# Layer 0's modulation products moved between the chunks of the first block's FFN, all modulation kept as columns

## The reference

```python
for l in range(DEPTH):                                   # DEPTH = 2
    mod_x = (silu(c) @ ada_w[l] + ada_b[l])[:, None, :]   # ada_w[l]: 1024 x 6144
    mod_c = silu(c_ctx) @ ada_w[l] + ada_b[l]
    sh1, sc1, g1, sh2, sc2, g2 = jnp.split(mod_x, 6, axis=-1)
    csh1, csc1, cg1, csh2, csc2, cg2 = jnp.split(mod_c, 6, axis=-1)
    hx = rms_norm(x, norm_g[l, 0]) * (1 + sc1) + sh1
    ...
    x = x + g1 * rms_norm(yx, norm_g[l, 1])
```

## Time and profile before

| | us |
|---|---|
| median of 3 runs | 3338.43 |
| lowest, highest | 3336.55, 3341.86 |
| the profiled execution | 3342.58 |
| its span in the trace | 3340.4 |
| PE busy in it | 2973.3 (89%) |
| DVE busy | 1865.6 (56%) |
| ACT busy | 1396.6 (42%) |

### The profile page before, as it was taken

The page is one execution under the profiler, slowest core; times in us unless marked ns, Lnnn a source line. Parts: engine busy times, 40 slices in busy tenths (PEclk is TensorE's granted clock), DMA queues, the critical chain, the costliest instruction groups (busy, mean ns, idle before and its releaser), DMA issues. The chain is left out here.

```text
span 3340.4 us, 38468 instructions
## 1 busy us (share of the span) xinstructions
PE 2973.3 (89%) x15372; PEld 2271.3 (68%) x15372; DVE 1865.6 (56%) x2265; ACT 1396.6 (42%) x1786; POOL 13.5 (0%) x13
## 2 busy tenths in 40 slices
PE   6999599795899999999999789999778998889797
PEld 4799498675667676676676544548667776757796
DVE  3555444334788887888888530205444554345675
ACT  3211244232666666676666411213133333343554
POOL 0000000000000000000000000000000000000000
PEclk9999799897899999999999888899679999999898
DMA  4300245331798898998899895120012222210352
GB/s 156 135 1 1 76 152 183 133 114 66 297 350 331 339 350 320 348 347 329 340 352 344 321 420 197 57 76 4 1 51 84 88 89 76 88 45 20 122 188 76
DMA packets 95036, 589.98 MB, mean 177 GB/s; under 512 B 20464, under 2 KB 21488, under 8 KB 25488
## 3 DMA queue, kind: packets, MB, share of 16 engines
q1 hardware_dynamic: 91840, 581.22, 46.4%
q10 hardware_dynamic: 3024, 6.33, 0.5%
HBM read 586.46 MB, written 1.05 MB: 176 GB/s over the span
## 5 line engine op out<-in xcount | busy, mean ns | idle before, releaser
L1807 DVE TENSOR_TENSOR s_w_low<-weight_ring,s_w_high 128x2048 fp32r<-128x2048 f32 x336 | 759.6, 2289 | 136.9 <-ACT s_w_high L1746 133.0
L1746 ACT ACTIVATE s_w_high<-weight_ring 128x2048 fp32r<-128x2048 f32 x336 | 629.7, 1908 | 139.1 <-PE bank L1727 116.5
L248 DVE TENSOR_TENSOR s_w_low<-weight_ring,s_w_high 128x1024 fp32r<-128x1024 f32 x238 | 289.3, 1221 | 200.0 <-ACT s_w_high L233 199.9
L1727 PE MATMUL bank<-s_w_high,s_x_low 128*96 128x512 f32 x896 | 364.1, 406 | 7.6 <-DVE s_w_low L1807 7.6
L233 ACT ACTIVATE s_w_high<-weight_ring 128x1024 fp32r<-128x1024 f32 x238 | 249.6, 1052 | 282.8 <-PE bank L490 282.8
L490 PE MATMUL bank<-s_x_high,s_w_low 128*128 128x256 f32 (+1 forms) x1056 | 341.1, 323 | 29.4 <-DVE s_w_low L248 29.4
L1727 PE MATMUL bank<-s_w_high,s_x_high 128*96 128x512 f32 x896 | 359.1, 401 | 0.0
L1727 PE MATMUL bank<-s_w_low,s_x_high 128*96 128x512 f32 x896 | 357.3, 399 | 0.0
L490 PE MATMUL bank<-s_x_low,s_w_high 128*128 128x256 f32 (+1 forms) x1056 | 339.5, 321 | 0.0
L490 PE MATMUL bank<-s_x_high,s_w_high 128*128 128x256 f32 (+1 forms) x1056 | 339.2, 321 | 0.0
L344 PE MATMUL bank<-s_w_high,s_x_low 128*128 128x512 f32 x544 | 220.2, 405 | 56.8 <-DVE s_w_low L248 56.8
(11 more groups left out here) (437 smaller groups left out, 4297.6 us busy)
## 6 DMA issues: line engine op xcount, KB each, us to landing
weight_ring<-moe_w SPq DMA_DIRECT2D x336, 1024.0 KB, 6.3
weight_ring<-ada_w SPq DMA_DIRECT2D x48, 1024.0 KB, 12.8
weight_ring<-ffn_up SPq DMA_DIRECT2D x44, 1024.0 KB, 4.8
weight_ring<-ffn_w_in SPq DMA_DIRECT2D x22, 1024.0 KB, 4.8
weight_ring<-ffn_down SPq DMA_DIRECT2D x22, 1024.0 KB, 4.8
weight_ring<-ffn_w_down SPq DMA_DIRECT2D x11, 1024.0 KB, 4.8
weight_ring<-w_rkv_cols SPq DMA_DIRECT2D x8, 1024.0 KB, 8.2
weight_ring<-moba_qk SPq DMA_DIRECT2D x8, 1024.0 KB, 4.8
```

What stands on the lines that cost most here:

```text
L248: K.nc.vector.tensor_tensor(self.lo[:, b, :], self.source(c, i), self.hi[:, b, :], ALU.subtract)\
L1727: last = nc.tensor.matmul(o, xs[:, e % 2, k, :], ws[:, b, c], start=(k == 0 and m == 0), stop=(k == KT - 1 and m == 2))
L1746: nc.scalar.activation(halves(whi, kind, n, i), raw(kind, n, i), ACT.Copy).then_inc(S["high"].h, 1)
L1807: V.tensor_tensor(halves(wlo, kind, n, i), raw(kind, n, i), halves(whi, kind, n, i), ALU.subtract)\
```

## The change

1. The 24 chunks of layer 0 are taken out of `adaln` and put into the FFN phase, two after each group's up chunk, and four after the last group. The step's products run between the groups on PE (`steps[0]`), ACT copies the bank after the next silu (`steps[1]`), and every vector, gates included, is turned to columns by four matmuls a step. The columns are kept in `modulation_columns`.
2. For this, the FFN's two outputs of a chunk share one bank (the other banks go to the modulation), and a chunk's four parts run in another order: both halves of the rows for the first 128 outputs, then for the second.
3. silu of the conditions is formed at the head of the FFN phase, and their load is issued as the program's first DMA; both leave `moe`.
4. `adaln` keeps 12 steps (layer 1), with the gates first (`KIND`). The repeated bias and gain rows are no longer loaded: gates are added and multiplied as columns (8 values wide), and a row is then made by 8 matmuls of a repeated column against the identity (`row`) and two copies by DVE (`keep`). PE waits for the small loads before its first step, for the gate columns after the step b = 2, for kept rows at b = 4 and b = 7. The layer norm's square roots are asked from ACT after its copies b = 2 and b = 3. The modulation of the transposed tokens is put into the copy out of the bank.
5. A small table and two small buffers of a later stage are laid over `modulation_columns` and `condition_wide`.

```diff
--- before.py
+++ after.py
@@ gated_hidden, tensor
                 for s in range(2):
-                    for i in range(2):
-                        pe.wait_ge(*parts.low.at(4 * c + 2 * s + i + 1))
+                    for n in range(4):
+                        i, h = (n % 2, n // 2) if steps else (n // 2, n % 2)
+                        if n == 0 or (i and n < 3):
+                            pe.wait_ge(*parts.low.at(4 * c + 2 * s + i + 1))
...
+                        if h:
+                            last.then_inc(*(K.used if i else parts.half).up())
                     K.taken += 1
+                if steps:
+                    for b in (c,) if c < chunks - 1 else (c, c + 1):
+                        steps[0](pe, b)
+            if steps:
+                steps[0](pe, None)
@@ gated_hidden, scalar
+            if steps:
+                steps[3](act)
             for q in range(0, KT, 2):
                 nc.scalar.activation(xhi[:, q:q + 2, :], x[:, q:q + 2, :], ACT.Copy).then_inc(*xsplit.up())
...
                     last.then_inc(*gated.up())
+                    if steps and c:
+                        steps[1](act, c - 1)
@@ modulation_steps
+    def tensor(pe, b):
+        if b == 0:
+            pe.wait_ge(*cond_made.at(1))
+        if b is not None:
+            if b >= 2:
+                pe.wait_ge(*copied.at(b - 1))
+            for c in range(2):
+                w = K.chunk(pe).rearrange("p (k n) -> p k n", k=KT)
+                for k in range(KT):
+                    r = slice(k % 4 * 32, k % 4 * 32 + 32)
+                    last = nc.tensor.matmul(K.ps[4 + b % 2][r, c * 256:c * 256 + 256], K.wide[:, k, :], w[:, k, :],
+                                            start=(k < 4), stop=(k >= 4))
+                last.then_inc(*K.used.up())
+        n = 11 if b is None else b - 1
...
+        pe.wait_ge(*copied.at(n + 1))
+        for j in range(4):
+            o = 8 * n + 2 * j
+            last = nc.tensor.matmul(K.ps[6][:, o:o + 2], mod[:, n % 2, j * P:(j + 1) * P], K.pick[:, :],
+                                    start=True, stop=True)
+        last.then_inc(*spread.up())
...
+    def begin(act):
+        act.wait_ge(*cond_in.at(16))
+        nc.scalar.activation(K.wide[:, :, 0:2], K.cond[:, :, :], ACT.Silu).then_inc(*cond_made.up())
@@ adaln, tensor
+                def row(r, bank):
+                    for h in range(2):
+                        for m in range(4):
+                            j = 4 * h + m
+                            last = nc.tensor.matmul(K.ps[bank + h][:, m * P:(m + 1) * P],
+                                                    bc(gcol[:, r, j:j + 1], [P, P]), K.ident[:, :], start=True, stop=True)
+                        last.then_inc(*row_made.up())
+
+                pe.wait_ge(*cols_in.at(48))
...
+                    if b:
+                        columns(b - 1)
+                    if b == 2:
+                        pe.wait_ge(*gates_made.at(1))
+                        row(0, 0)
+                        row(1, 2)
+                    if b == 4:
+                        pe.wait_ge(*row_kept.at(2))
+                        row(2, 0)
+                        pe.wait_ge(*row_kept.at(4))
+                        row(3, 2)
+                    if b == 7:
+                        pe.wait_ge(*row_kept.at(8))
+                        turn(0)
+                        turn(1)
@@ adaln, scalar
-                root_of_norm(0)
-                for b in range(24):
+                for b in range(12):
...
+                    if b in (2, 3):
+                        root_of_norm(b - 2)
+                    if b == 4:
                         square(2, 0)
                         square(3, 1)
@@ adaln, sync
-                for n in range(4):
-                    load(K, sp, grb[:, n, :], i["ada_b_gates"][n].partition_broadcast(P))
-                    load(K, sp, gng[:, n, :], i["norm_g_gates"][n].partition_broadcast(P))
@@ build
-        chunks("ffn_w_in")
+        for c in range(FF // 256):
+            chunks("ffn_w_in", 2 * c, 2 * c + 2)
+            chunks("ada_w", 2 * c, 2 * c + 2)
+        chunks("ada_w", 22, 24)
...
-        chunks("ada_w")
+        for kind in (2, 5, 0, 1, 3, 4):
+            chunks("ada_w", 24 + 4 * kind, 28 + 4 * kind)
```

More of the change, by code:

```diff
@@ L195, with __init__ @@
 class Split:
-    def __init__(self, K, st, chunks, depth, rows=None):
-        self.K, self.first, self.rows = K, K.taken, rows
+    def __init__(self, K, st, chunks, depth, rows=None, where=lambda c: c):
+        self.K, self.first, self.rows, self.where = K, K.taken, rows, where
         self.chunks, self.depth, self.nact, self.ndve = chunks, depth, 0, 0
@@ L212, in source @@
     def source(self, c, i):
-        return self.K.ring[:, (self.first + c) % R, i * CH // 2:(i + 1) * CH // 2]
+        return self.K.ring[:, (self.first + self.where(c)) % R, i * CH // 2:(i + 1) * CH // 2]
     def at(self, c, i):
@@ L223, in act @@
             c = self.nact
-            n = self.first + c
+            n = self.first + self.where(c)
             act.wait_ge(K.landed[n % R], 16 * (n // R + 1))
@@ L228, in act @@
                 if c >= self.depth:
-                    act.wait_ge(*(K.used if i else self.half).at(c - self.depth + 1))
+                    act.wait_ge(*(K.used.at(self.where(c - self.depth) + 1) if i else self.half.at(c - self.depth + 1)))
                 if self.rows:
@@ L452, in layer_norm, with gated_hidden @@
         K.v(dve, nc.vector.tensor_tensor(flat, flat, b, ALU.add))
-def gated_hidden(K, st, x, hid, chunks, conv=None):
+def gated_hidden(K, st, x, hid, chunks, conv=None, steps=None):
     nc = K.nc
@@ L465, in gated_hidden @@
     centre, tapped, gated, free, xsplit, xlow = K.sig(6)
-    parts = Split(K, st, 2 * chunks, 1 if tok > T else 2)
+    where = (lambda c: c + 2 * (c // 2)) if steps else (lambda c: c)
+    parts = Split(K, st, 2 * chunks, 1 if tok > T else 2, where=where)
     K.uniq += 1
@@ L527, in _ @@
                 silu(chunks - 1)
+            if steps:
+                steps[1](act, chunks - 1)
+                steps[1](act, chunks)
         @block.vector
@@ L536, in product @@
                 last.then_inc(*free.up())
+            if steps:
+                steps[4](dve)
             for q in range(0, KT, 2):
@@ L561, in _ @@
                 product(chunks - 1)
+            if steps:
+                steps[2](dve)
             dve.wait_ge(*free.now())
@@ L566, in _, with modulation_steps, scalar, pick @@
             K.stream(sp)
+def modulation_steps(K, st, first):
+    nc = K.nc
+    V = nc.vector
+    cond_in, cond_made, picked, copied, spread = (K.early[n] for n in ("cond_in", "cond_made", "picked", "copied", "spread"))
+    mod, = scratch(K, st, [P, 2, 512])
+    out = K.columns[:, 0].rearrange("p q j w -> p (q j w)")
+    def tensor(pe, b):
[12 more added lines that the diff above has]
+        n = 11 if b is None else b - 1
+        if n < 0:
+            return
+        if n == 0:
+            pe.wait_ge(*picked.at(1))
+        pe.wait_ge(*copied.at(n + 1))
[4 more added lines that the diff above has]
+        last.then_inc(*spread.up())
+    def scalar(act, b):
+        act.wait_ge(*K.used.at(2 * min(b, 10) + 2 + 2 * b + 2))
+        if b >= 2:
+            act.wait_ge(*spread.at(b - 1))
+        nc.scalar.activation(mod[:, b % 2, :], K.ps[4 + b % 2][:, :], ACT.Copy).then_inc(*copied.up())
+    def pick(dve):
+        for who in range(2):
+            last = V.reduce_sum(K.pick[:, who:who + 1],
+                                K.ident[:, :].rearrange("p (q n) -> p n q", q=4)[:, who:who + 1, :], AX)
+        K.v(dve, last, picked)
+    def vector(dve):
+        dve.wait_ge(*spread.at(12))
+        K.v(dve, V.tensor_copy(out, K.ps[6][:, 0:96]))
+    def begin(act):
+        act.wait_ge(*cond_in.at(16))
+        nc.scalar.activation(K.wide[:, :, 0:2], K.cond[:, :, :], ACT.Silu).then_inc(*cond_made.up())
+    return tensor, scalar, vector, begin, pick
 def rwkv_front(K, units, cols, bones, hsel, bonus, dstate, edge, loads):
@@ L1920, in root_of_norm @@
                     nc.scalar.activation(rs[:, :], rs[:, :], ACT.Sqrt).then_inc(*norm_root.up())
[L1922 to L1923 removed]
+                for b in range(12):
                     act.wait_ge(*K.used.at(2 * b + 2))
[L1925 to L1930 removed]
+                    if b == 8:
+                        act.wait_ge(*spread.at(8))
+                        for n in range(2):
+                            last = nc.scalar.activation(K.columns[:, 1, 2 + 3 * n, :, :].rearrange("p j w -> p (j w)"),
+                                                        K.ps[6][:, 32 + 48 * n:48 + 48 * n], ACT.Copy)
+                        last.then_inc(*shifted.up())
+                    if b >= 2:
+                        act.wait_ge(*spread.at(b - 1))
+                    nc.scalar.activation(mod[:, b % 2, :], K.ps[4 + b % 2][:, :], ACT.Copy).then_inc(*copied.up())
+                    if b in (2, 3):
+                        root_of_norm(b - 2)
```

(3 more changed lines are left out.)

279 lines of the change are left out of this document (140 added, 139 removed).

## The result

| | us |
|---|---|
| before, median of 4 runs (lowest, highest) | 3339.66 (3336.55, 3341.86) |
| after, median of 4 runs (lowest, highest) | 3308.93 (3303.17, 3313.85) |
| ratio, with its 95% interval | 0.9905 (0.9890 to 0.9921) |
| profiled executions, before and after | 3342.58, 3303.17 |
| their spans | 3340.4, 3301.3 |

The forecast was 3313 with a range of 3301 to 3327. The four runs lie in two pairs, 3303 and 3304 against 3313 and 3314, and the profile is of a run of the lower pair. The profiled difference, 39.4 us, is therefore more than the medians' 30.7.

The account below looks back on a forecast made before the run. The prediction took `adaln` to be bound by weight transfers and the FFN by PE. Its terms, 35.1 - 59 - 1.3 = -25.2 us, took the profiled 3342.58 to 3317.4, or a median of 3313, range 3301 to 3327.

Parts of the forecast that it names:

- The FFN, +35.1: FFN phase: PE has no idle time, so the added matmuls lengthen it by 35.1 us, head, seams and tail included.
- head: Start of the FFN phase: ACT's table load and silu of the conditions before x is split, +1.5 us.
- seams: FFN: 23 changes between fp32r and step matmuls, 0.5 us allowed in all, 2.3 if each cost 0.1 us.
- tail: End of the FFN phase: DVE's last product is covered, a copy of 96 values takes its place, -0.5 us.
- `adaln`, -59: `adaln`: a chain of waits among PE, ACT and DVE replaces the transfer bound, ending at 76.4 us; 59 us shorter.
- Small terms, -1.3: Outside FFN and `adaln`: conditions' load leaving a list -0.45, exp table load running ahead -1.3, program's first DMA +0.5 us.
- The router stage: Router's phase: conditions' load leaves a waited list, -0.45 us, and exp's table load no longer waits for DVE, -1.3 us.
- The program's start: Program's head: the conditions' load is the first DMA, so all behind it comes 0.45 us later, taken as +0.5.
- The clock in the FFN: Rival: thin steps lower PE's clock at FFN seams; 3373 us for the whole (3%), 3344 for steps only (4%).
- The chain's slow end: Rival in `adaln`: waits invite the slow clock, gain of 43 us in place of 59, 3329 us; 13%.
- the fast end: Rival in `adaln`: the clock rises early and stays, gain of 67 us, 3305 us; 10%.
- The ring: Rival in the FFN: the third close transfer lands 1 us late in every group, 3324 us; reserve about 8 us, 2%.

Follow-up runs that it names:

- e5: The kernel before the change, unaltered, run and profiled again: 3343.52 us.
- e11: The kernel before the change with 25 DVE memsets (3.11 us) added at the end of the router's phase: 3340.63 us.
- the repeat: The changed kernel, unaltered, run again: median of four runs 3302.11 us, ratio 0.9879 to the kernel before.
- e4: The changed kernel with the four column matmuls of each of the FFN's twelve steps made four times over: 3363.26 us.
- e6: The changed kernel with the layer norm's two square roots in `adaln` asked one step earlier: 3296.93 us in one run.
- e7: The changed kernel with PE's wait for the bias columns in `adaln`, and the bias matmul, moved behind the second step: 3309.72 us in one run.

## Why the prediction was right

**The FFN, +35.1: measured +35.0.** From the start of the transposition phase to the next phase's first matmul it was 144.3 us (413.66 to 557.95), now 179.3 (415.67 to 594.96). The parts: head 10.80 against 9.42, +1.4 (forecast 1.5); from the first FFN matmul to PE's end +34.5 (forecast 33.6, and 0.5 of seams); tail 4.72 against 5.56 of waiting, -0.8 (-0.5). A step is 1.86 and 0.92 us, as sized from `adaln`; each seam to and from an fp32r matmul costs 0.08 to 0.09 us over their regular 0.12. That is some 1.9 us for 23 seams, the mis-sized term here: near the 2.3 that the prediction named as the alternative, and not the 0.5 that it took. What offset it is luck: behind the first FFN matmul PE ran at 1.2 GHz for 4.0 us and not for 5.3, which gave back 0.65. The sum is sounder than its first decimal, though: the phase is 143.7 to 144.3 us in the four profiles without the move, and 178.8 to 179.5 in the eight with the phase as in after. The groups are 14.45 us apart (products at 453.50 and 467.95), 14.3 by the forecast.

**`adaln`, -59: measured -64.7.** The chain was the right one, link for link, with no wait for `ada_w`. Most links were forecast a little long, in us from the start of the phase:

| | forecast | measured |
|---|---|---|
| first step | 3.9 | 3.3 |
| step 2's products done | 13 | 11.1 |
| first root | 15.4 | 13.3 |
| first norm | 19 | 17.0 |
| gate columns | 20.8 | 18.5 |
| rows 0 and 1 | 26.8 | 24.5 |
| second root | 29.8 | 27.1 |
| second norm, four copies | 36.2 | 33.4 |
| rows 2 and 3, step 5 | 43 | 39.6 |
| squares | 46.3 | 42.5 |
| kept rows | 50.4 | 46.2 |
| PE's end | 74.1 | 69.8 |
| last coefficient | 76.4 | 71.3 |

No link is far off, and nearly all errors have one sign. The largest is the first three steps, 7.8 us instead of 9: the slow clock cost less there than I took (64 records in 4.93 us, then one step at 1.93). The start is 0.6 us shorter. The root, from the products' end to its own, is 2.2 us for 2.4. The strings of tiny DVE operations start 0.1 to 0.2 us apart, so twelve coefficients take 1.5 us, not 2.3. For the rows 0 and 1 the slow clock was sized well (5.95 us, 6 forecast), and so was PE alone at the end (23.6, 23.7). One error cost nothing: DVE places a half tile in 1.3 us (16 operations in 5.20) and not in 0.9, which is slower than `turn`, but a step stands between the two pairs of `turn` and hides it.

**Small terms, -1.3.** The router stage gave -2.6 for -1.8. The mechanism is seen (the table load at 855.19 ahead of its wait), but the size is not fixed: the nine kernels with this edit and no memsets have 185.1 to 187.9 us there, and without the time at 1.2 GHz, taken off as above, the edit is worth 0.3 to 1.3 us. The program's start was +0.5 in the forecast; the first `ffn_w_in` is issued at 139.75, 140.36 and 140.30 in the three profiles of the kernel before (e5 and e11 with it), and at 139.42 to 141.04 in the eleven of the others, 140.4 in the mean: +0.2, with more scatter than size.

**The sum.** The three places together are 35.0 - 64.7 - 2.6 + 0.2 = -32.1 where -25.2 was forecast. That puts the median at 3306.3, between the two that were measured, 3308.9 and 3302.1. The profile's other 7 us come from stages and parts of stages that were not touched: -10.4 in three stages, and +3.3 in the first one ahead of the FFN and behind it. There the clock falls elsewhere. No step of the prediction had them. So the mechanism and the direction of each term are the prediction's merit; that the first median came within 4 us is in part luck, since the repeat is 11 us under the forecast and 1 us inside the stated range, which reached so far down only because `adaln`'s bounds were wide.

**The rivals.** The clock in the FFN did not fall; that it can, e4 shows. The chain's slow end did not come. The gain, 64.7, is nearer to the fast end's 67 than to the forecast's 59.5, but not by the fast end's reason: the clock was not at 2.4 GHz throughout (0.83 from 1933 to 1953 us), the links were shorter. The ring was in time for PE at every seam, with less in hand than the 8 us of the forecast: ACT waited for the next gate chunk's transfer in eight groups, the longest time 7.91 us, and then DVE ended its split at 538.29 us, 4.7 us before PE took it.

## What to carry to other kernels

Move weights from a stage that is bound by transfers into one that is bound by PE, and price each added matmul at its full time there; what the first stage gives back is the length of the chain that then remains, which has to be followed link by link. Keep thin matmuls between dense ones short: 1.0 us of them cost only themselves, 3.7 us also the clock behind them, at six seams of ten. And where a gap of 1.7 us brings the clock down in one run and not in another, read a change of some us in its own stage, and take the time at 1.2 GHz off before two profiles are compared; in the total a gain of 7 us can vanish.

## What the hardware showed that I had not expected

- The same gap of 1.72 us, in the same code, was followed by a fall of the clock to 1.2 GHz in one program and not in another (1.5 us each time). 1.84 us of memsets ahead of the stage went with two more such falls.
- Stages far from an edit take one of several lengths (the even layer 200.9, 202.8 to 203.5, 204.7 or 205.9 to 206.1 us), and the first stage, which no edit of e6 or e7 precedes, 695.3 and 705.2 us on one chip. Without the time at 1.2 GHz the even layer is 192.8 or 192.9 us in all fourteen profiles.
- 3.7 us of matmuls with two output columns, with PE never idle, brought the clock down at six seams and not at four.
